# RoPE's row exchange in two projection stages: copies issued by GpSimd before, a permutation matmul after

## The reference

```python
def _partial_rope(t, cos, sin):
    half = ROT_DIM // 2                      # ROT_DIM = 16
    x1 = t[..., :half].astype(jnp.float32)
    x2 = t[..., half:ROT_DIM].astype(jnp.float32)
    r1 = (x1 * cos - x2 * sin).astype(t.dtype)
    r2 = (x2 * cos + x1 * sin).astype(t.dtype)
    return jnp.concatenate([r1, r2, t[..., ROT_DIM:]], axis=-1)
```

## Time and profile before

| | |
|---|---|
| median of 3 runs | 1969.36 us (1964.46 to 1973.93) |
| profiled execution | 1964.46 us, its span 1962.7 us |
| TensorE busy | 1843.0 us (94%) |
| VectorE busy | 1064.1 us (54%) |
| ScalarE busy | 833.5 us (42%) |
| GpSimd busy | 163.4 us (8%) |
| mean granted TensorE clock | 0.979 |

### The profile page before, as it was taken

How to read it: one execution, slowest core, us unless ns; L and a number is a source line. 1 busy time by engine, 2 the same in 40 slices (tenths; PEclk the granted TensorE clock), 3 DMA queues, 4 the chain that set the end, 5 groups by cost and what they waited for, 6 DMA issues and landing times.

```text
span 1962.7 us, 24252 instructions
## 1 busy us (share of the span) xinstructions
PE 1843.0 (94%) x8916; PEld 1422.7 (72%) x8916; DVE 1064.1 (54%) x1640; ACT 833.5 (42%) x1393; POOL 163.4 (8%) x228
## 2 busy tenths in 40 slices
PE   6887999999999879989999999989999989999997
PEld 3676878888888656657888888868666667866665
DVE  7695454444333657756444443475555376555437
ACT  4221334444322556744344422233566533365653
POOL 7542000000000000000000000023000002200000
PEclk9888999999999999999999999999999999999999
DMA  4311222232333111102222233323111122311111
GB/s 173 103 46 44 96 87 97 95 99 96 96 98 99 50 30 29 58 33 97 97 96 96 96 89 99 102 81 103 55 54 52 35 86 84 100 54 50 48 36 61
DMA packets 58876, 152.16 MB, mean 78 GB/s; under 512 B 17281, under 2 KB 22177, under 8 KB 58785
## 3 DMA queue, kind: packets, MB, share of 16 engines
q1 hardware_dynamic: 55232, 148.25, 23.7%
q0 software_dynamic: 3552, 2.70, 0.5%
HBM read 143.77 MB, written 4.19 MB: 75 GB/s over the span
## 4 chain that ended last, share of the span: by engine, by line
PE 85%; DVE 9%; ACT 4%; issue 2%; DMA 0%; POOL 0%; DVEq 0%; SPq 0%; ACTq 0%
PE bank L1840 18%; PE bank L1841 18%; PE bank L1842 18%; PE bank L2312 3%; PE bank L2314 3%; PE bank L2313 3%; PE bank L2289 2%; PE bank L2277 1%; PE bank L2275 1%; PE bank L2276 1%; PE bank L2045 1%; DVE wl L1100 1%; PE bank L2073 1%; ACT wh L595 1%; PE bank L2399 1%
## 5 line engine op out<-in xcount | busy, mean ns | idle before, releaser
L1100 DVE TENSOR_TENSOR wl<-raw,wh 128x1024 fp32r<-128x1024 f32 (+3 forms) x280 | 324.3, 1158 | 531.0 <-ACT wh L595 528.4
L595 ACT ACTIVATE wh<-raw 128x1024 fp32r<-128x1024 f32 (+3 forms) x280 | 279.1, 997 | 602.9 <-PE bank L1842 510.4
L1840 PE MATMUL bank<-xH,wh 128*128 128x512 f32 x896 | 352.6, 394 | 8.5 <-DVE wl L1100 6.6
L1841 PE MATMUL bank<-xL,wh 128*128 128x512 f32 x896 | 349.9, 391 | 0.0
L1842 PE MATMUL bank<-xH,wl 128*128 128x512 f32 x896 | 349.8, 390 | 0.0
L1840 PEld LDWEIGHTS bank<-xH,wh 128*128 128x128 f32 x896 | 169.1, 189 | 48.2 <-issue 9.8
L1841 PEld LDWEIGHTS bank<-xL,wh 128*128 128x128 f32 x896 | 168.9, 189 | 35.9 <-issue 1.1
L1842 PEld LDWEIGHTS bank<-xH,wl 128*128 128x128 f32 x896 | 168.9, 188 | 35.2
L1840 PE MATMUL bank<-hidH,wh 128*128 128x512 f32 x352 | 137.3, 390 | 0.0
L1842 PE MATMUL bank<-hidH,wl 128*128 128x512 f32 x352 | 136.9, 389 | 0.0
L1841 PE MATMUL bank<-hidL,wh 128*128 128x512 f32 x352 | 136.9, 389 | 0.0
(11 more groups left out here) (425 smaller groups left out, 3313.6 us busy)
## 6 DMA issues: line engine op xcount, KB each, us to landing
raw<-w_gu_dram SPq DMA_DIRECT2D x88, 512.0 KB, 3.4
raw<-w_p_dram SPq DMA_DIRECT2D x64, 512.0 KB, 3.4
raw<-w_dn_dram SPq DMA_DIRECT2D x32, 448.0 KB, 3.3
raw<-w_glu_dram SPq DMA_DIRECT2D x16, 512.0 KB, 3.5
raw<-w_dn_dram SPq DMA_DIRECT2D x16, 512.0 KB, 3.6
raw<-w_out_dram SPq DMA_DIRECT2D x16, 512.0 KB, 3.5
raw<-w_in_dram SPq DMA_DIRECT2D x8, 512.0 KB, 7.4
raw<-w_o_dram SPq DMA_DIRECT2D x8, 512.0 KB, 3.4
```

The source lines that it names most:

```text
L595: nc.scalar.activation(wh[:, (st.base + u) % 2, 0:kts * P], raw[:, (st.base + u) % 4, 0:kts * P], ACT.Copy).then_inc(w_high, 1)
L1100: nc.vector.tensor_tensor(wl[:, s, 0:kts * P], raw[:, (st.base + u) % 4, 0:kts * P], wh[:, s, 0:kts * P].bitcast(F32), ALU.subtract).then_ ...
L1840: nc.tensor.matmul(bank, wh[:, s, w], hi[:, k, :], start=first and kt == 0, stop=False)
L1841: nc.tensor.matmul(bank, wh[:, s, w], lo[:, k, :], start=False, stop=False)
```

## The change

A constant matrix `rotate` (128 x 128, of zeros and ones) is added to `cons`: used as the stationary operand, it puts row j + 8 in row j and row j in row j + 8 for the first 16 rows of each head, and zero in the rest. TensorE applies it to each evicted tile in fp32, into bank 4 or 5, and VectorE multiplies the bank by `rope_sin`. GpSimd's 64 copies and their semaphores are gone; its loads of the cosine and sine rows stay. TensorE's wait for the last `roped` stands before the second half of stage `v`, since that half writes banks 4 and 5.

```diff
@@ constants
-for _n, _w in (("ident", P), ("ones", P), ("from_here", P), ("minus8", P), ("causal", P),
+for _n, _w in (("ident", P), ("ones", P), ("rotate", P), ("from_here", P), ("minus8", P), ("causal", P),
@@ GpSimd
-                    pool.dma_start(to, con[:, CON[name][0]:CON[name][1]]).then_inc(sem("rope_rows1"), 16)
-                for n in range(8):
-                    slot = n if n < 4 else n + 4
-                    pool.wait_ge(evicted, tiles[f"qk{layer}"] + n + 5)
-                    if n >= 2:
-                        pool.wait_ge(sem("roped"), 8 * layer + n - 1)
-                    elif n == 1:
-                        pool.wait_ge(sem("rope_rows1"), 288 * layer + 32)
-                    for at, source in ((0, 8), (8, 0), (HEAD, HEAD + 8), (HEAD + 8, HEAD)):
-                        pool.dma_start(exchanged(n)[at:at + 8, :], qk[source:source + 8, slot, :]).then_inc(sem(f"rope_rows{n % 2}"), 16)
+                    pool.dma_start(to, con[:, CON[name][0]:CON[name][1]]).then_inc(sem("rope_loaded"), 16)
@@ VectorE, rope(n)
-                    dve.wait_ge(sem(f"rope_rows{n % 2}"), (288 * layer + 32 if n % 2 else 256 * layer) + 64 * (n // 2 + 1))
-                    step(nc.vector.tensor_tensor(sd[:, :], exchanged(n), rope_sin, ALU.mult))
+                    dve.wait_ge(sem("rotated"), 8 * layer + n + 1)
+                    step(nc.vector.tensor_tensor(sd[:, :], banks[4 + n % 2][:, :], rope_sin, ALU.mult))
@@ TensorE, stage qk
+                def rotate(n):
+                    pe.wait_ge(evicted, tiles[f"qk{layer}"] + n + 5)
+                    if n >= 2:
+                        pe.wait_ge(sem("roped"), 8 * layer + n - 1)
+                    nc.tensor.matmul(banks[4 + n % 2][:, :], const("rotate"), qk[:, n if n < 4 else n + 4, :], start=True, stop=True)\
+                      .then_inc(sem("rotated"), 1)
+
                 for n in range(8):
...
                         product(st, n // 4, n % 4, xH, xL, o)
+                    if n:
+                        rotate(n - 1)
@@ TensorE, stage v
                             if k == 0 and j == 0 and half:
+                                pe.wait_ge(sem("roped"), 8 * layer + 8)
                                 pe.wait_ge(sem("fz_ready"), layer + 1)
...
                     ins.then_inc(w_used, 1)
+                    if n == 0:
+                        rotate(7)
@@ TensorE, ahead of the attention steps
-                pe.wait_ge(sem("roped"), 8 * layer + 8)
```

More of the change, by code:

```diff
@@ L326, in out_bank @@
         return banks[(tiles[f"out{layer}"] + n) % 4 if n else 7][:, :]
-    def exchanged(n):
-        return sq[:, 1, :] if n % 2 else acc[:, :]
     def q_scale(slot):
@@ L1683, in rope @@
                     if n == 0:
-                        dve.wait_ge(sem("rope_rows1"), 288 * layer + 32)
+                        dve.wait_ge(sem("rope_loaded"), 32 * (layer + 1))
                     tile = qk[:, n if n < 4 else n + 4, :]
-                    dve.wait_ge(sem(f"rope_rows{n % 2}"), (288 * layer + 32 if n % 2 else 256 * layer) + 64 * (n // 2 + 1))
-                    step(nc.vector.tensor_tensor(sd[:, :], exchanged(n), rope_sin, ALU.mult))
+                    dve.wait_ge(sem("rotated"), 8 * layer + n + 1)
+                    step(nc.vector.tensor_tensor(sd[:, :], banks[4 + n % 2][:, :], rope_sin, ALU.mult))
                     step(nc.vector.tensor_tensor(tile, tile, rope_cos, ALU.mult))
@@ L2524, in _constants @@
     put("fold", (i >= DN) & (i % DR == j % DR))
+    head, dim, half = j // 64, j % 64, 8
+    source = np.where(dim < half, j + half, j - half)
+    put("rotate", (dim < 2 * half) & (i == source))
     put("from_here", np.where(i >= j, -8.0, 0.0))
```

## The result

| | before | after |
|---|---|---|
| median | 1969.36 us | 1982.36 us |
| lowest to highest, 5 runs each | 1964.46 to 1973.93 | 1979.64 to 1986.06 |
| profiled execution, its span | 1964.46, 1962.7 | 1985.31, 1983.5 |
| TensorE busy | 1843.0 us | 1860.6 us |
| GpSimd busy | 163.4 us | 131.8 us |

A forecast was written before the change was run, and what follows sets the result against it. TensorE, busy 94% of the span, was taken to set the end. Removed copies and added waits counted 0; 16 rotates at 0.87 us add 13.9 to the median 1969.36, giving 1983.3 us (+0.7%), range 1975 to 1991.

The forecast's parts named there:

- What bounds the stage: Stage `qk`: TensorE is busy 44.00 of 44.00 us, so there is no gap for one more matmul.
- What goes is worth 0: Rotary step in both layers: GpSimd's 64 copies, about 15.8 us of its time a layer, delay nobody; removal gains 0.
- The price of one rotate, 0.87 us: TensorE, `qk` and `v`: each fp32 matmul of 512 columns costs 0.87 us, as line 2013; 16 make 13.9 us.
- Nothing is hidden, and no added wait holds: `qk` and `v`: no idle time absorbs the matmuls, and the added waits for evictions, banks, `rotated` and `roped` cost 0.
- The small things: VectorE reading PSUM instead of SBUF costs 0; `cons` growing by 64 KB costs 0, 1.4 us at most if uncovered.
- Rival 1: Exchange matmuls on TensorE run at the fp32 transposes' rate, 0.44 us each: +7.0, 1976.4 us; chance 7%.
- Rival 2: Each rotate falls into TensorE idle time at the edge between two tiles: price 0, 1969.4 us; chance 3%.
- Rival 3: TensorE's sequencer stops at each added wait, each rotate costing near 1.2 us: 19.2 us more, 1988.6 us; chance 8%.
- Rival 4: `rotated` comes after VectorE's turn, the split is late and TensorE stands before each product: +30, 1999 us; chance 2%.
- The two base times: Whole kernel: profiled execution 1964.46 us, giving 1978.4, or the three runs' median 1969.36, giving 1983.3; forecast used the median.

The follow-up runs named there:

- experiment 1: The kernel before, unchanged, timed and profiled once more: ratio 0.9993 to the kernel before, median 1968.96 us.
- experiment 2: The kernel before without GpSimd's 64 copies, the exchange of rows left out: ratio 0.9998 to the kernel before, median 1969.53 us.
- experiment 8: The kernel after, unchanged, timed again beside the kernel before: ratio 1.0071, median 1984.40 us.
- experiment 6: The kernel after with the exchange matmuls in fp32r, ScalarE evicting each tile a second time, rounded: ratio 1.0017 to the kernel before, median 1973.04 us.
- experiment 3: The kernel after with GpSimd's copies back and read by VectorE, the 16 matmuls made but unread: ratio 1.0073 to the kernel before, median 1983.95 us.
- experiment 5: The kernel before with 128 more columns of unread zeros in the constants loaded at the start: ratio 0.9996, median 1968.91 us.
- experiment 7: The kernel before with two of G's five operations ahead of a weight block's split at the start and three behind it: ratio 0.9972, median 1963.91 us.

## Why the prediction was right, step by step

- *What bounds the stage.* Right. The `qk` window was full before and is full after, and what was added to TensorE came out in the time whole: TensorE's busy time, forecast to rise by about 14 us, is 14.6 above that of experiment 1.
- *What goes is worth 0.* Right: experiment 2, ratio 0.9998 and tiles 5.44 us apart.
- *The price of one rotate, 0.87 us.* The form was right, the size 0.04 too small. I subtracted two steps as 0.23 where a plain step is 5.44 / 24 = 0.227, and closed the window at the second matmul behind. The steps that follow are 0.23 to 0.24 as well before they are back at 0.227, as 1316.42 to 1316.65 above. From tile to tile the price is 0.91: 0.86 of passes and 0.05 once. The sum should have been 14.6. The four steps of 0.23, 0.92 in all, which the prediction set above the trace, were nearer than its 0.87. Against the profile of experiment 1, which like most executions is not one of the short ones, the stages give 14.4; the medians gave 13.0 and then 14.2, and both intervals hold 14.6. That the forecast's 13.9 lies only 0.9 from the first result is partly luck: the price was too small, and the first five runs gave 13.0 where experiment 8's gave 14.2.
- *Nothing is hidden, and no added wait holds.* Right, by the idle times of 0.0 ahead of lines 2231 and 1675.
- *The small things.* Right: the bank operand 682 ns, the constants 0.9996.
- *Rival 1, a cheap matmul.* Out. A rotate costs 0.91 us although its matrix is of zeros and ones, and in fp32r (experiment 6) 0.23 us, as the products beside it. The rows that the rival rests on are `transpose` calls, and a rotate is a `matmul` call; no run made the exchange with the former.
- *Rival 2, not slower.* Out: experiment 3 has the whole loss.
- *Rival 3, a dear matmul.* Out: 0.91 was measured and not 1.2, and the same waits stand before the fp32r one, which costs 0.23.
- *Rival 4, a broken pipeline.* Out: VectorE's turn came right behind the split as before, which starts at 1316.74 and takes 1.23 us, with line 1675 at 1317.88 in the profile after.
- *The two base times.* The forecast stood on the median and not on the profiled execution, 4.9 us below it. Had it stood on the profiled one, 1978.4 us, it would have been under the lowest run after.

## What to carry to other kernels

Where TensorE is busy for all of a window, as in `qk` here, expect a matmul to cost its full spacing whatever idle engine it relieves; GpSimd's copies were free, since nobody waited for them. Read the price from the distance of two whole tiles with and without the operation, not from its neighbours' starts. Before comparing two profiles, look at the first stage that neither kernel changed: here it held 4.8 us of a difference of 20.8.

## What the runs showed of the hardware

The start's length follows the order in which two instructions begin. VectorE's split of a weight block (line 1100) and first operation of G (line 1140) meet GpSimd's line 529 there; all three have both inputs in SBUF. In the first profile both of VectorE's begin first:

```profile
53.76 1.22 DVE L1100 TENSOR_TENSOR wl<-raw,wh 128x1024 fp32r<-128x1024 f32 x1 [0.46 <-ACT wh L595]
54.90 1.27 DVE L1140 TENSOR_TENSOR tv<-pf,Bz 128x1024 f32<-128x1024 f32 x1
...
55.28 2.68 POOL L529 TENSOR_TENSOR Er<-Er,sm 128x1024 f32<-128x1024 f32 x1 [0.18 <-POOL sm L502]
```

In experiment 1 GpSimd's begins first, and VectorE's two take 5.4 us in place of 2.5, GpSimd's 1.92 in place of 2.68:

```profile
54.63 2.49 DVE L1100 TENSOR_TENSOR wl<-raw,wh 128x1024 fp32r<-128x1024 f32 x1 [0.46 <-ACT wh L595]
57.05 2.93 DVE L1140 TENSOR_TENSOR tv<-pf,Bz 128x1024 f32<-128x1024 f32 x1
60.02 1.22 DVE L1140 TENSOR_TENSOR G<-bank,Bz 128x1024 f32<-128x1024 f32 x1
...
54.13 1.92 POOL L529 TENSOR_TENSOR Er<-Er,sm 128x1024 f32<-128x1024 f32 x1 [0.18 <-POOL sm L502]
...
58.98 3.25 POOL L531 TENSOR_TENSOR Er<-Er,tp 128x1024 f32<-128x1024 f32 x1
```

All ten profiles follow this (line numbers differ a little between kernels), and there are three cases. GpSimd's first: the split takes 2.12 to 2.50 us, and the state-space stage starts at 89.6 to 90.3 us (seven profiles). GpSimd's between VectorE's two: 1.22 or 1.23 us, then 2.94 (experiment 5, 88.4 us, and experiment 7 with its other order). GpSimd's last: 1.22 and 1.27, 85.0 us (the first profile alone). VectorE's operation with one input in a bank takes 1.22 or 1.23 us in all of them, though an operation of GpSimd runs beside it. That the short runs of the two series are those of the third case is likely, and not shown: only one short run was profiled.

When the five operations of G are late, so is the split behind them that TensorE waits for, and behind the gap the granted clock falls: it is 0.76 of full speed over 70 to 80 us in experiment 1, its lower level, 1.2 GHz, for a part of them. The Trainium skill (SBUF — State Buffer, who interferes with whom) states that a VectorE instruction with two inputs in SBUF contends with a GpSimd instruction that reads SBUF, and that the order of issue decides which of them blocks. These rows agree, and the operation with an input in a bank, never stretched, does not speak against it. No run here took GpSimd's operations away, so that the cause is argued and not shown.
